# One attention stage reordered: B's logits computed once, C's and D's branches set between A's transposes and values

## The chip, the core and the metric

The kernel runs on one core of a Trainium2 chip. Each of the core's engines runs its own list of instructions: TensorE (PE in the rows; PEld is its weight load), VectorE (DVE), ScalarE (ACT), GpSimd (POOL) and SyncE (SP), which issues most of the DMAs. They meet only at semaphores. The metric is the device time of one execution in microseconds (us); lower is better.

## The reference, cut to what matters

Two layers of a decoder trunk, for a prompt of 512 tokens and 8 sample tokens that share the weights. Four branches read the same normalised input. Each is projected to 1024 features, multiplied by its own sigmoid gate (a 1024 x 1024 projection for each branch), and the four are summed.

```python
# A: four query heads, two key/value heads; the top 128 keys of each query are kept
score = einsum('bth,bthl->btl', iw, relu(einsum('bthd,bld->bthl', iq, kidx)))
_, idx = top_k(score, topk)
p = softmax(where(selected, q @ k * 64**-0.5, NEG)); o_a = p @ v
# B: stick-breaking, four heads
z = einsum('bthd,blhd->bhtl', q, k) * 64**-0.5
log_keep = where(mask, log_sigmoid(-z), 0)
after = cumsum(log_keep, reverse) - log_keep
a = where(mask, exp(log_sigmoid(z) + after), 0); o_b = a @ v
# C and D are scans over chunks; they are finished before the stage that is changed here
merged = g0*(o_a @ w_br_a) + g1*(o_b @ w_br_b) + g2*(o_c @ w_br_c) + g3*(o_d @ w_br_d)
```

B's exponent is `z` plus a reverse cumulative sum of the masked softplus of `z`, taken negative.

## The kernel before

Everything is float32. A dense tile of weights (1024 x 128) is split in a leading part (ACT, line 1018, in `WH`) and a rest (DVE or POOL, lines 1321 and 1745, in `WL`), and `dense_split` multiplies 8 chunks by 3 products by 2 halves of 260 tokens, 48 matmuls (line 490). Weights arrive in a ring of four slots; a slot is free when PE has counted `tile_used`.

The stage that the change touches is the prompt's attention, once in each layer. Its loop runs over t = 0 to 3. In step t, A handles the 128 queries of block t against w = 128 (t + 1) keys, and B handles its head t for all 512 queries, as four blocks of keys (`bblock`, 512, 384, 256 and 128 columns wide). Between these PE computes the gates of C and D for two chunks of 128 features (four `gate_cd`, into PSUM banks 2 and 3) and the matching projections of C and D (four `branch_cd`, into the same two banks). All orders are written out by hand, each engine's as a list with waits.

PE's order in step t: four index products (line 844); B's logits (851); two of A's logits (`attend`, 859); `gate_cd` 0 and 1; a wait for the masked softplus; the cumulative sums of B (869, 871), each followed by the logits of the block once more, added to the same bank (851); `gate_cd` 2; B's values (880); A's two other logits; `gate_cd` 3; four `branch_cd` (825); then for each head of A the transposes of its probabilities (897), and one head behind them its values (543).

The partners: ACT takes relu of the index products (1187), computes B's softplus term in three passes (1190 to 1192), B's weights (1199), A's exponentials (1204), the gates' tanh (1208), and copies A's transposed probabilities back for PE (1220). DVE forms the index score (1619, 1622), finds the top 128 in 16 rounds of max and replace (1650, 1651; none in step 0), adds up the softplus (1633, seen as line 1300), scales the gates out of banks 2 and 3 (`gate_cd_scaled`, 1613, seen as line 1297), finishes A's softmax, and multiplies each `branch_cd` by its gate out of the same banks (1668, seen as 1300). So each `gate_cd` waits for DVE to have taken the one before (`f_raw`), and each `branch_cd` for DVE to have taken the one before (`f_used`). In the 16 rounds, the softplus stands ahead of round 5, and the scalings of gates 0 and 1 ahead of rounds 7 and 12:

```python
for k in range(TOPK_P // 8):
    if k == 5:
        softplus()
    elif k == 7:
        gate_cd_scaled(t, 0)
    elif k == 12:
        gate_cd_scaled(t, 1)
    do(v_.max(M8[:, :], score))
    do(v_.match_replace(score, M8[:, :], score, TAKEN))
```

In step 0 DVE also rebuilds the rest part `XL` of the normalised input, eight operations on 128 x 520, because the scans before have used its memory. POOL masks (1732, 1793), splits weights (1745) and adds C and D (1807).

Of the kernel before, what the change touches and what calls it, by code (L numbers as in the profile page):

```python
# [11 lines left out]
NPR = 512  # L12
# [4 lines left out]
KD = DM // 128  # L17
# [79 lines left out]
def trunk_kernel(nc, x_in, pages, consts, vecs, states, c_state, d_state, k_c, v_c,  # L97
# [9 lines left out]
    with ctx:  # L107
# [373 lines left out]
        def _(pe):  # L481
# [54 lines left out]
            def values(l, t, h):  # L536

                q0 = 64 * (h // 2)
                if t and h == 0:
                    pe.wait_ge(*a_out.nth(l, t - 1))  # L540
                pe.wait_ge(*at_trc.nth(l, 4 * t + h))
                for j in range(t + 1):
                    ins = mm(PS[q0:q0 + 64, 6, 256 + 128 * (h % 2):384 + 128 * (h % 2)], TM[:, T_AV, j, q0:q0 + 64],
                             PTR[h % 2][:, 128 * j:128 * j + 128], start=j == 0, stop=j == t)
                finish(ins, at_pv)
# [23 lines left out]
            for l in range(L):  # L569
# [246 lines left out]
                def branch_cd(t, i):  # L816
                    nb = FIRST["fill"] + 5 * t + 4
                    if i == 0:
                        pe.wait_ge(*full(l, nb))
                        pe.wait_ge(*f_raw.nth(l, 4 * t + 3))  # L820
                    else:
                        pe.wait_ge(*f_used.nth(l, 4 * t + i - 1))
                    for k in range(2):
                        for a in range(2):
                            ins = mm(PS[:, 2 + a, 0:HALF],  # L825
                                     slot(l, nb)[:, 256 * i + 128 * k:256 * i + 128 * k + 128],
                                     F[:, (CQ, DZ)[i % 2] + k, a * HALF:(a + 1) * HALF], start=k == 0, stop=k == 1)
                    finish(ins, tile_used if i == 3 else f_done)
# [4 lines left out]
                for s in (c_out, d_out):  # L833
                    pe.wait_ge(*s.nth(l, 1))
                for t in range(NT):
# [14 lines left out]
                    def logits(i, start):  # L850
                        return mm(bblock(i), F[r0:r0 + 64, BK + c, 128 * i:128 * i + 128],  # L851
                                  F[r0:r0 + 64, BQ + c, 128 * i:NPR], start=start, stop=True)
                    for i in range(NT):
                        ins = logits(i, True)
                    finish(ins, z_done)

                    def attend(h):
                        q0 = 64 * (h // 2)
                        finish(mm(PS[:, h % 2, 0:w], F[q0:q0 + 64, AQ + h % 2, 128 * t:128 * t + 128],
                                  F[q0:q0 + 64, AK, 0:w], start=True, stop=True), at_qk)  # L860
# [7 lines left out]
                    for i in range(NT):  # L868
                        mm(bblock(i), kc(C_NTRI), BA1[:, OFF[i]:OFF[i] + NPR - 128 * i], start=True, stop=False)
                        for j in range(i + 1, NT):  # L870
                            mm(bblock(i, 128 * (j - i)), kc(C_NONE),
                               BA1[:, OFF[j]:OFF[j] + NPR - 128 * j], start=False, stop=False)
                        ins = logits(i, False)
# [13 lines left out]
                    for i in range(4):  # L887
                        branch_cd(t, i)
                    for h in range(4):
                        q0 = 64 * (h // 2)  # L890
# [9 lines left out]
                        if h:  # L900
                            values(l, t, h - 1)
                    values(l, t, 3)
# [78 lines left out]
        def _(act):  # L981
# [42 lines left out]
            for l in range(L):  # L1024
# [157 lines left out]
                for t in range(NT):  # L1182
# [18 lines left out]
                    split(l, m + 4)  # L1201
                    for h in range(4):
                        act.wait_ge(*at_max.nth(l, 4 * t + h))
                        do(A(S[:, h, 0:w], S[:, h, 0:w], ACT.Exp, bias=MX[:, h:h + 1], scale=0.125,
                             accum_out=MX[:, 4 + h:5 + h]), at_exp)
                    for i in range(4):
                        act.wait_ge(*f_raw.nth(l, 4 * t + i))
                        do(A(gate_at(t, i), gate_at(t, i), ACT.Tanh, scale=0.5), f_tanh)
                    split(l, m + 5)
                    if t % 2:  # L1210
                        act.wait_ge(*pv_done.nth(l, t))
                        do(A(F[:, BQ + t // 2, 0:NPR], PS[:, 7, :], ACT.Copy), b_out)
                    if t == 0:
                        act.wait_ge(stored.sem, N_STORES_MID[l])
# [72 lines left out]
        def _(dve):  # L1287
# [76 lines left out]
            for l in range(L):  # L1364
# [249 lines left out]

                for t in range(NT):
# [8 lines left out]
                    if t == 0:  # L1624
                        for k in range(KD):
                            stt(XL[:, k, :], X[:, k, :], V[:, l, V_NPRE + k:V_NPRE + k + 1], XH[:, k, :].bitcast(f32),
                                ALU.mult, ALU.subtract, xl_again)
# [14 lines left out]
                    else:  # L1642
                        for k in range(TOPK_P // 8):
                            if k == 5:
                                softplus()
                            elif k == 7:
                                gate_cd_scaled(t, 0)
                            elif k == 12:
                                gate_cd_scaled(t, 1)
# [320 lines left out]
```

## Time and profile before

| | |
|---|---|
| median of 3 runs | 2766.27 us (2757.04 to 2773.68) |
| the profiled execution: its own time | 2763.92 us |
| its span, first to last instruction | 2762.2 us |
| mean granted TensorE clock (1 is 2.4 GHz, 0.5 is 1.2 GHz) | 0.912 |
| PE busy | 2428.7 us (88%) |
| DVE, ACT, POOL busy | 1417.8 (51%), 904.2 (33%), 345.9 us (13%) |
| attention stage of layer 0, of layer 1 | about 497.8 to 766.0, 1869.6 to 2138.0 us from the start |

Busy time of PE is that of overlapping, pipelined matmuls, so 88% is no peak. In rows in order of time, the number in square brackets is how long the engine sat idle before the group, with what released it.

### The profile page before, as it was taken

To read this page: it belongs to the slowest core of one execution; us is meant where nothing else is said; L and a number is where in the kernel's file an instruction comes from. 1 tells how busy PE (TensorE), PEld (TensorE's weight loads), DVE (VectorE), ACT (ScalarE), POOL (GpSimd) and SP (SyncE) were. 2 spreads that over 40 slices of the span, in tenths; PEclk is the share of its full clock that TensorE was granted. 3 is DMA by queue.
4 is the path that set the end of the run, shared out by engine and by line. 5 is a ranking of instruction groups with operands and counts; after the bars stand their busy time and mean duration, and the time that the engine had idled before them with its cause. 6 is when DMAs were issued, how large, how long until landed. Compare 5 with 4: busy or idle time off the path is not lost.

```text
span 2762.2 us, 40540 instructions
## 1 busy us (share of the span) xinstructions
PE 2428.7 (88%) x15956; PEld 2022.7 (73%) x15956; DVE 1417.8 (51%) x2215; ACT 904.2 (33%) x1288; POOL 345.9 (13%) x412
## 2 busy tenths in 40 slices
PE   6899778788899899999898996987888997999996
PEld 6659424566699789989784683345666997999896
DVE  3329444445634577772342484444455445777723
ACT  3023424333322444442220225133333224444421
POOL 0016132222200000000000251222222000000000
PEclk9999658899999899999999996578999998999998
DMA  4362330111122122222215424201111221222221
GB/s 156 116 205 83 109 126 1 49 47 39 39 77 92 54 85 93 92 93 79 104 65 161 151 72 144 85 0 57 46 39 39 85 85 62 79 91 92 93 85 62
DMA packets 85184, 229.85 MB, mean 83 GB/s; under 512 B 10498, under 2 KB 28034, under 8 KB 84354
## 3 DMA queue, kind: packets, MB, share of 16 engines
q1 hardware_dynamic: 72434, 204.16, 22.3%
q10 hardware_dynamic: 12560, 23.11, 2.6%
q8 instruction: 126, 2.06, 0.3%
q14 instruction: 64, 0.52, 0.1%
HBM read 216.68 MB, written 10.55 MB: 82 GB/s over the span
## 4 chain that ended last, share of the span: by engine, by line
PE 73%; DVE 15%; ACT 6%; DMA 2%; issue 2%; ACTq 1%; POOL 1%; SPq 0%; DVEq 0%; POOLq 0%
PE PS L490 49%; PE PS L968 3%; PE PS L825 2%; DVE T L1425 2%; DVE M L1424 2%; DMA R<-k_c 2%; DVE S L1300 2%; DVE F L1300 2%; PE PS L782 1%; PE PS L851 1%; PE PS L555 1%; PE PS L522 1%; PE PS L919 1%; PE PS L718 1%; DVE WL L1321 1%
## 5 line engine op out<-in xcount | busy, mean ns | idle before, releaser
L490 PE MATMUL PS<-XH,WH 128*128 128x260 f32 x3616 | 760.6, 292 | 114.9 <-DVE WL L1321 43.4
L490 PE MATMUL PS<-XL,WH 128*128 128x260 f32 x3616 | 741.0, 287 | 5.3 <-issue 5.3
L490 PE MATMUL PS<-XH,WL 128*128 128x260 f32 x3616 | 740.0, 287 | 0.0
L490 PEld LDWEIGHTS PS<-XH,WH 128*128 128x128 f32 x3616 | 576.9, 194 | 133.8 <-issue 93.0
L1018 ACT ACTIVATE WH<-R 128x1024 fp32r<-128x1024 f32 x270 | 286.0, 1059 | 1043.1 <-PE PS L490 848.9
L490 PEld LDWEIGHTS PS<-XL,WH 128*128 128x128 f32 x3616 | 570.6, 193 | 5.7 <-issue 5.7
L490 PEld LDWEIGHTS PS<-XH,WL 128*128 128x128 f32 x3616 | 569.7, 193 | 0.0
L1321 DVE TENSOR_TENSOR WL<-R,WH 128x1024 fp32r<-128x1024 f32 x204 | 250.8, 1230 | 386.3 <-ACT WH L1018 385.5
L1745 POOL TENSOR_TENSOR WL<-R,WH 128x1024 fp32r<-128x1024 f32 x66 | 156.6, 2373 | 467.5 <-ACT WH L1018 466.7
L490 PE MATMUL PS<-FR,WH 128*128 128x260 f32 x1024 | 186.3, 284 | 0.0
L1297 DVE TENSOR_TENSOR S<-PS,RB 128x520 f32<-128x520 f32 x120 | 83.9, 700 | 176.0 <-PE PS L490 174.4
L490 PEld LDWEIGHTS PS<-FR,WH 128*128 128x128 f32 x1024 | 150.1, 189 | 0.1
L1300 DVE SCALAR_TENSOR_TENSOR S<-S,V 128x510 f32<-128x510 f32 (+1 forms) x176 | 132.2, 751 | 6.2
L1297 DVE TENSOR_TENSOR F<-PS,RB 128x520 f32<-128x520 f32 x56 | 39.2, 700 | 150.2 <-PE PS L490 149.6
L1741 POOL TENSOR_SCALAR F<-F 128x1040 f32<-128x1040 f32 x2 | 5.7, 2852 | 773.8 <-DVE F L1297 773.8
L825 PE MATMUL PS<-F,R 128*128 128x260 f32 x256 | 64.4, 395 | 28.9 <-DVE F L1300 21.3
L968 PE MATMUL PS<-F,R 128*128 128x260 f32 x384 | 87.5, 383 | 0.8 <-PE PS L968 0.8
L1424 DVE MAX8 M<-T 8x8 f32<-8x1025 f32 x64 | 77.9, 1217 | 19.6 <-ACT T L1051 17.4
L968 PEld LDWEIGHTS PS<-F,R 128*128 128x128 f32 x384 | 71.5, 190 | 11.6 <-issue 1.6
L825 PEld LDWEIGHTS PS<-F,R 128*128 128x128 f32 x256 | 46.0, 189 | 45.8 <-DVE F L1300 31.1
L1425 DVE MATCH_REPLACE8 T<-M,T 8x1025 f32<-8x1025 f32 x64 | 76.8, 1200 | 0.0
L1264 ACT ACTIVATE S<-S,V 128x520 f32<-128x520 f32 x88 | 72.5, 824 | 3.2
(306 smaller groups left out, 2901.4 us busy)
## 6 DMA issues: line engine op xcount, KB each, us to landing
R<-w_up SPq DMA_DIRECT2D x88, 512.0 KB, 3.2
R<-w_gate SPq DMA_DIRECT2D x64, 512.0 KB, 3.2
R<-w_proj SPq DMA_DIRECT2D x58, 512.0 KB, 3.2
R<-v_c SPq DMA_DIRECT2D x128, 192.0 KB, 2.4
R<-w_down SPq DMA_DIRECT2D x44, 512.0 KB, 3.2
R<-k_c SPq DMA_DIRECT2D x72, 256.0 KB, 3.2
R<-k_c ACTq DMA_DIRECT2D x56, 256.0 KB, 3.6
R<-w_br SPq DMA_DIRECT2D x16, 512.0 KB, 3.2
```

What stands on the lines that cost most here:

```text
L490: i = mm(PS[:, bank + a, 0:HALF], p[:, w, k * 128:(k + 1) * 128], x[:, a * HALF:(a + 1) * HALF], start=first and p is WH and x is hi, stop ...
L522: ins = mm(PS[:, 4 + a, 0:HALF], kc(C_ONE), S[:, k % 2, a * HALF:(a + 1) * HALF], start=k == 0, stop=k == KD - 1)
L825: ins = mm(PS[:, 2 + a, 0:HALF], slot(l, nb)[:, 256 * i + 128 * k:256 * i + 128 * k + 128], F[:, (CQ, DZ)[i % 2] + k, a * HALF:(a + 1) * H ...
L968: ins = mm(PS[:, bank + a, 0:HALF], slot(l, n)[:, 128 * e:128 * e + 128], F[:, q, a * HALF:(a + 1) * HALF], start=k == 0, stop=k == JF - 1)
L1018: do(A(WH[:, half(l, m), :], slot(l, SPLIT[m]), ACT.Copy), w_hi)
L1264: do(A(S[:, 2 + g, :], S[:, g, :], ACT.Identity, bias=V[:, l, V_FCB + ch:V_FCB + ch + 1], scale=V[:, l, V_FCW + 3 * ch + 2:V_FCW + 3 * ch ...
L1297: do(v_.tensor_tensor(out, a, b, op), s)
L1300: do(v_.scalar_tensor_tensor(out, a, sc, b, o0, o1), s)
L1321: v_.tensor_tensor(WL[:, half(l, m), :], slot(l, SPLIT[m]), WH[:, half(l, m), :].bitcast(f32), ALU.subtract).then_inc(w_lo.sem, 1)
L1424: do(v_.max(M8[0:8, :], T[0:8, 0:PAST + 1]))
L1425: do(v_.match_replace(T[0:8, 0:PAST + 1], M8[0:8, :], T[0:8, 0:PAST + 1], TAKEN))
L1745: g_.tensor_tensor(WL[:, half(l, m), :], slot(l, SPLIT[m]), WH[:, half(l, m), :].bitcast(f32), ALU.subtract).then_inc(w_lo_p.sem, 1)
```

## The change

It has six parts. (1) In the cumulative sums, B's logits are not computed a second time: the sums are added onto the logits that have stood in the banks since the start of the step. (2) A's heads are walked in another order, so that neighbours in the loop lie in different halves of the partitions: `attend` takes rows 0 to 63 and 64 to 127 in turn, and `values` handles two heads at once, whose matmuls alternate between output partitions 0 to 63 and 64 to 127. (3) PE's tail of a step becomes: branch 0, transposes of two heads, branch 1, values of these two, branch 2, transposes of the other two, branch 3, their values. (4) ACT computes tanh of gates 0, 1 and 2 ahead of A's exponentials or between them, and B's output copy and the next split ahead of tanh of gate 3. (5) In DVE's rounds, softplus stands ahead of round 4, gates 0 and 1 ahead of rounds 5 and 10. (6) DVE rebuilds `XL` before the loop, and PE waits for the outputs of C and D at the first `branch_cd` and no longer before the loop.

```diff
-            def values(l, t, h):
-                q0 = 64 * (h // 2)
-                if t and h == 0:
+            def values(l, t, p):
+                if t and p == 0:
                     pe.wait_ge(*a_out.nth(l, t - 1))
-                pe.wait_ge(*at_trc.nth(l, 4 * t + h))
+                for h in range(2 * p, 2 * p + 2):
+                    pe.wait_ge(*at_trc.nth(l, 4 * t + h))
                 for j in range(t + 1):
-                    ins = mm(PS[q0:q0 + 64, 6, 256 + 128 * (h % 2):384 + 128 * (h % 2)], TM[:, T_AV, j, q0:q0 + 64],
-                             PTR[h % 2][:, 128 * j:128 * j + 128], start=j == 0, stop=j == t)
-                finish(ins, at_pv)
+                    for h in range(2 * p, 2 * p + 2):
+                        q0 = 64 * (h % 2)
+                        ins = mm(PS[q0:q0 + 64, 6, 256 + 128 * p:384 + 128 * p], TM[:, T_AV, j, q0:q0 + 64],
+                                 PTR[h % 2][:, 128 * j:128 * j + 128], start=j == 0, stop=j == t)
+                        if j == t:
+                            finish(ins, at_pv)
...
                 def branch_cd(t, i):
...
+                        if t == 0:
+                            pe.wait_ge(*c_out.nth(l, 1))
+                            pe.wait_ge(*d_out.nth(l, 1))
...
                 pe.wait_ge(*scaled.nth(l, 1))
-                for s in (c_out, d_out):
-                    pe.wait_ge(*s.nth(l, 1))
...
-                        q0 = 64 * (h // 2)
-                        finish(mm(PS[:, h % 2, 0:w], F[q0:q0 + 64, AQ + h % 2, 128 * t:128 * t + 128],
+                        q0 = 64 * (h % 2)
+                        finish(mm(PS[:, h % 2, 0:w], F[q0:q0 + 64, AQ + h // 2, 128 * t:128 * t + 128],
...
                     for i in range(NT):
-                        mm(bblock(i), kc(C_NTRI), BA1[:, OFF[i]:OFF[i] + NPR - 128 * i], start=True, stop=False)
+                        ins = mm(bblock(i), kc(C_NTRI), BA1[:, OFF[i]:OFF[i] + NPR - 128 * i], start=False,
+                                 stop=i == NT - 1, skip_group_check=True)
                         for j in range(i + 1, NT):
-                            mm(bblock(i, 128 * (j - i)), kc(C_NONE),
-                               BA1[:, OFF[j]:OFF[j] + NPR - 128 * j], start=False, stop=False)
-                        ins = logits(i, False)
+                            ins = mm(bblock(i, 128 * (j - i)), kc(C_NONE),
+                                     BA1[:, OFF[j]:OFF[j] + NPR - 128 * j], start=False, stop=j == NT - 1,
+                                     skip_group_check=True)
                     finish(ins, ac_done)
...
-                    for i in range(4):
-                        branch_cd(t, i)
-                    for h in range(4):
-                        q0 = 64 * (h // 2)
+                    def turn(h):
                         pe.wait_ge(*at_norm.nth(l, 4 * t + h))
...
                         finish(ins, at_tr)
-                        if h:
-                            values(l, t, h - 1)
-                    values(l, t, 3)
+                    branch_cd(t, 0)
+                    turn(0)
+                    turn(1)
+                    branch_cd(t, 1)
+                    values(l, t, 0)
+                    branch_cd(t, 2)
+                    turn(2)
+                    turn(3)
+                    branch_cd(t, 3)
+                    values(l, t, 1)
...
+                    gate_cd_tanh(0)
+                    gate_cd_tanh(1)
                     for h in range(4):
+                        if h == 2:
+                            gate_cd_tanh(2)
                         act.wait_ge(*at_max.nth(l, 4 * t + h))
...
-                    for i in range(4):
-                        act.wait_ge(*f_raw.nth(l, 4 * t + i))
-                        do(A(gate_at(t, i), gate_at(t, i), ACT.Tanh, scale=0.5), f_tanh)
-                    split(l, m + 5)
                     if t % 2:
                         act.wait_ge(*pv_done.nth(l, t))
                         do(A(F[:, BQ + t // 2, 0:NPR], PS[:, 7, :], ACT.Copy), b_out)
+                    split(l, m + 5)
+                    gate_cd_tanh(3)
...
+                for k in range(KD):
+                    stt(XL[:, k, :], X[:, k, :], V[:, l, V_NPRE + k:V_NPRE + k + 1], XH[:, k, :].bitcast(f32),
+                        ALU.mult, ALU.subtract, xl_again)
                 for t in range(NT):
...
                         for k in range(TOPK_P // 8):
-                            if k == 5:
+                            if k == 4:
                                 softplus()
-                            elif k == 7:
+                            elif k == 5:
                                 gate_cd_scaled(t, 0)
-                            elif k == 12:
+                            elif k == 10:
                                 gate_cd_scaled(t, 1)
```

## Rows read from the trace of the kernel before

**Rows 1.** The page's chain that ended last, share of the span by engine.

```profile
PE 73%; DVE 15%; ACT 6%; DMA 2%; issue 2%; ACTq 1%; POOL 1%; SPq 0%; DVEq 0%; POOLq 0%
```

**Rows 2.** Stretches: length, busy us of PE, PEld, DVE, ACT, POOL (instructions), clock, DMA.

```profile
497.80:766.00 268.20, 223.49 (x1267) 176.37 (x1268) 137.20 (x303) 95.02 (x156) 63.62 (x62) 0.93 0.14 47
1869.60:2138.00 268.40, 223.86 (x1266) 176.45 (x1267) 137.21 (x303) 95.01 (x156) 63.61 (x62) 0.93 0.14 47
```

**Rows 3.** The chain in order of time, layer 0, step 1: start, us, what.

```profile
595.02 1.05 PE PS L851 x2
...
600.30 0.42 PE PS L851 x2
600.72 5.95 PE PS L490 x48
```

**Rows 4.** PE in order of time: first matmuls of gate 1, steps 1 to 3.

```profile
584.64 0.80 PE L490 MATMUL PS<-XH,WH 128*128 128x260 f32 x2 [4.58 <-DVE F L1297]
...
648.17 0.80 PE L490 MATMUL PS<-XH,WH 128*128 128x260 f32 x2 [4.79 <-DVE F L1297]
...
715.16 0.80 PE L490 MATMUL PS<-XH,WH 128*128 128x260 f32 x2 [6.51 <-DVE F L1297]
```

**Rows 5.** DVE in order of time: softplus in step 1, four rows of step 3.

```profile
579.82 2.06 DVE L1300 SCALAR_TENSOR_TENSOR F<-PS,F 128x512 f32<-128x512 f32 x4 [1.51 <-ACT F L1192]
...
709.27 2.07 DVE L1300 SCALAR_TENSOR_TENSOR F<-PS,F 128x512 f32<-128x512 f32 x4
...
714.41 0.70 DVE L1297 TENSOR_TENSOR F<-PS,RB 128x520 f32<-128x520 f32 x1
...
733.49 0.15 DVE L1303 TENSOR_SCALAR MX<-MX 128x1 f32<-128x1 f32 x1
```

**Rows 6.** PE in order of time: tail of step 0, tail of step 3.

```profile
555.92 1.99 PE L825 MATMUL PS<-F,R 128*128 128x260 f32 x8 [0.95 <-DVE F L1297]
...
569.29 0.70 PE L844 MATMUL PS<-F 64*128 64x256 f32 x4
...
747.96 1.99 PE L825 MATMUL PS<-F,R 128*128 128x260 f32 x8 [0.96 <-DVE F L1297]
750.84 2.02 PE L825 MATMUL PS<-F,R 128*128 128x260 f32 x8 [0.89 <-DVE F L1300]
...
758.52 1.04 PE L897 MATMUL PS<-K,S 128*128 128x128 f32 x8
...
764.05 1.04 PE L543 MATMUL PS<-S,TM 128*64 128x128 f32 x8
```

**Rows 7.** PE in order of time: pairs in different halves, pairs in one half.

```profile
357.20 1.97 PE L714 MATMUL PS<-B,K 8*64 8x512 f32 x4 [10.83 <-POOL B L1764]
...
695.76 1.13 PE L844 MATMUL PS<-F 64*128 64x512 f32 x4
...
739.07 1.98 PE L859 MATMUL PS<-F 64*128 64x512 f32 x4
```

**Rows 8.** Stretches, columns as in Rows 2: during line 714's first pair.

```profile
357.20:359.10 1.90, 1.90 (x5) 0.29 (x5) 0.00 (x0) 1.87 (x3) 1.80 (x2) 0.50 0.00 0
```

**Rows 9.** DVE and POOL in order of time, start of the stage in layer 0.

```profile
512.18 3.22 DVE L1300 SCALAR_TENSOR_TENSOR F<-S,SMT,F 128x128 f32<-128x128 f32 x3
515.43 6.33 DVE L1300 SCALAR_TENSOR_TENSOR XL<-X,V,XH 128x520 fp32r<-128x520 f32 x8
...
523.39 2.07 DVE L1300 SCALAR_TENSOR_TENSOR F<-PS,F 128x512 f32<-128x512 f32 x4 [1.36 <-ACT F L1192]
...
509.71 4.76 POOL L1745 TENSOR_TENSOR WL<-R,WH 128x1024 fp32r<-128x1024 f32 x2 [22.78 <-ACT WH L1018]
```

**Rows 10.** PE in order of time: a pause in another stage, and the matmuls behind it.

```profile
1230.10 0.47 PE L490 MATMUL PS<-XH,WH 128*128 128x260 f32 x2 [3.43 <-DVE FR L1297]
...
1231.44 0.64 PE L490 MATMUL PS<-XH,WL 128*128 128x260 f32 x2
```

**Rows 11.** Stretches, columns as in Rows 2: gate 1 after its pause, step 1.

```profile
584.60:589.50 4.90, 4.86 (x22) 4.86 (x23) 4.57 (x15) 0.00 (x0) 1.24 (x1) 0.50 0.01 2
```

More of the change, by code:

```diff
@@ L848, in _ @@
                         pe.wait_ge(*a_out.nth(l, t - 1))
-                    def logits(i, start):
-                        return mm(bblock(i), F[r0:r0 + 64, BK + c, 128 * i:128 * i + 128],
-                                  F[r0:r0 + 64, BQ + c, 128 * i:NPR], start=start, stop=True)
                     for i in range(NT):
-                        ins = logits(i, True)
+                        ins = mm(bblock(i), F[r0:r0 + 64, BK + c, 128 * i:128 * i + 128],
+                                 F[r0:r0 + 64, BQ + c, 128 * i:NPR], start=i < 3, stop=True, skip_group_check=True)
                     finish(ins, z_done)
                     def attend(h):
-                        q0 = 64 * (h // 2)
-                        finish(mm(PS[:, h % 2, 0:w], F[q0:q0 + 64, AQ + h % 2, 128 * t:128 * t + 128],
+                        q0 = 64 * (h % 2)
+                        finish(mm(PS[:, h % 2, 0:w], F[q0:q0 + 64, AQ + h // 2, 128 * t:128 * t + 128],
                                   F[q0:q0 + 64, AK, 0:w], start=True, stop=True), at_qk)
@@ L1201, in _, with gate_cd_tanh @@
                     split(l, m + 4)
+                    def gate_cd_tanh(i):
+                        act.wait_ge(*f_raw.nth(l, 4 * t + i))
+                        do(A(gate_at(t, i), gate_at(t, i), ACT.Tanh, scale=0.5), f_tanh)
+                    gate_cd_tanh(0)
+                    gate_cd_tanh(1)
                     for h in range(4):
+                        if h == 2:
+                            gate_cd_tanh(2)
                         act.wait_ge(*at_max.nth(l, 4 * t + h))
@@ L1623, in _ @@
                             ix_sum if h == 3 else dve_own)
[L1624 to L1627, printed above, removed]
                     def softplus():
```

## The prediction

> **What bounds the kernel now.** First the chain of work that ended last: PE has 73% of it, DVE 15%, ACT 6% [rows 1]. So a change pays where it shortens PE's list, or a wait inside it. Then the stretches: the stage is as long in layer 1 as in layer 0, 268.4 and 268.2 us, and in both PE is busy for 223 us of it, DVE for 137, ACT for 95, at a granted clock of 0.93 [rows 2]. Two equal stages mean that one layer can be costed and doubled. Neither DVE nor ACT fills the stage, so PE sets the pace, and the 45 us in which it is idle are handovers to the other two. Third, PE in order of time shows where these lie. Gate 1 of steps 1 to 3 starts after pauses of 4.58, 4.79 and 6.51 us, each ended by DVE's line 1297, the scaling of gate 0 [rows 4]. Each branch after the first starts 0.89 us after the one before, waiting for DVE's product [rows 6]. Last, the chain in order of time passes through B's repeated logits, with nothing beside them [rows 3].
>
> **Logits once.** The reader should look at line 851 among the sums: 1.05 us for the block of 512 columns, 0.42 for that of 128 [rows 3]. Between them the cost is linear in columns, so four blocks take 4 x 0.735 = 2.94 us. The sums themselves stay, and whether they start a bank or add to it is the same number of matmuls. Behind them ACT and POOL prepare B's weights while PE runs gate 2, 5.95 us [rows 3]; both shift together, so no cover is lost. Gain: 2.94 a step.
>
> **Rounds 4, 5 and 10.** What PE waits for in gate 1 is softplus, two rounds, and the scaling. In step 1 softplus itself waited 1.51 us for ACT and began at 579.82 [rows 5], so a place one round ahead brings it no forward. But one round instead of two follows it: from its end, 581.88, to PE's start, 584.64, less a scaling of 0.70 and some 0.1 of handover, two rounds take 2.0 us. Gain 0.98. In step 3 softplus began without a wait [rows 5]: it moves up by one round, and one round less follows. Two rounds are 714.41 - 711.34 = 3.07 us. Gain 3.0 (1.5, should ACT's term come a round later than needed). Step 2 has rounds between these; its gain lies between one round and two, 1.25 and 2.5, of which I take 1.9.
>
> The price of the move is at the other end: six rounds instead of four now follow gate 1's scaling. In step 3 DVE had head 1's maximum at 733.64 [rows 5], and PE asked for it at 739.07 [rows 7]: 5.4 us of cover. PE is about to save 2.94 + 3.0 + 0.85 = 6.8 us ahead of that point, so there the cover goes and DVE decides. Gate 3 can't start before the maximum and gate 2's scaling, 733.64 + 0.70 = 734.34; it started at 741.05 [rows 7]. Step 3 can gain 6.7 at the most, and less by what DVE waits for gate 1 at round 10. With gate 1 partly at half clock, where 4.9 us cost 2.45 [rows 11], I put that wait between 0 and 1.6 and take 0.4: 6.3 for step 3 in all.
>
> **Pairs of logits.** Four 512-column matmuls whose inputs lie in two halves of the partitions take 1.13 us (line 844), and four in one half 1.98 (line 859) [rows 7]. The second pair of A's logits goes from the one kind to the other: 0.85 in step 3 (inside the 6.3), in proportion to columns 0.21, 0.43, 0.64 in steps 0 to 2. The first pair stands ahead of gate 0, and what it saves ends in gate 1's pause: nothing.
>
> **The tail.** From branch 0 to the next step's first product: 13.37 us in step 0 and, to the end of the last values at 765.08, 17.12 in step 3 [rows 6]; steps 1 and 2 in line with these, 14.6 and 15.9. New: four branches of 2.02 and three pauses of 0.89 [rows 6] make 10.75. Into the pauses go two heads' transposes, two heads' values, and two heads' transposes again. Eight transposes are 1.04 us in step 3, and one head's eight value matmuls 1.04 [rows 6]. If the values of two heads overlap, each of the pieces is 0.26 (t + 1): hidden in steps 0 to 2, 0.15 over in step 3. The last pair of values stays in the open. That is 11.0, 11.3, 11.5 and 12.2 us, a gain of 2.4, 3.3, 4.4 and 4.9. Each of the four pieces brings a handover that no row shows: between 0 and 0.4 us, twice the 0.2 that a pause of 0.89 leaves beside a product of 0.70 (the scaling's time for the same shape [rows 5]). I take 0.1 each, 1.6 a layer. The tail gives 15.0 - 1.6 = 13.4.
>
> Do the values overlap? The nearest rows are line 714's: four 512-column matmuls into two halves of the output in 1.97 us at half clock [rows 7, 8], against 1.98 at full clock for four in one half. At equal clock that is half the time. I take overlap.
>
> What stands in the queues: on ACT the copies of the transposed probabilities now lie behind a split and gate 3's tanh, but PE has a branch of 2.02 us to run before it needs them. The three tanh ahead of A's exponentials, some 2.1 us if each is like DVE's 0.70 on the same shape [rows 5], delay A's softmax under gate 3's 5.95. Without that cover they would delay the scaling of gate 3, and PE's first branch.
>
> **The start of the stage.** `XL` goes ahead of the score, 6.33 us of DVE [rows 9]. There it meets POOL's two splits, 4.76 us. Three 128-column operations beside these took 1.07 us each, more than the 0.79 of an `XL` operation four times as wide [rows 9], so DVE is held up by them. Held up for both, counted from POOL's start at 509.71, `XL` ends at 520.8 and the four score operations, at no more than 0.79 each, at 524.0; DVE waits for ACT's term until 523.39 anyway [rows 9]. So at worst 0.6 us shows, and I take nothing. The splits may wait in turn for one `XL` operation each: 0 taken, 1.6 a layer at most. PE's earlier start gains nothing, since ACT's relu still waits for D's output.
>
> **Sum of a layer.** Steps 0 to 3 ahead of the tail: 2.94 + 0.21 = 3.15; 2.94 + 0.98 + 0.43 = 4.35; 2.94 + 1.9 + 0.64 = 5.48; 6.3. Together 19.3, with the tail 32.7, twice 65.4. The profiled execution took 2763.92 us: 2698.5. The median of the runs lies 2.4 above the profiled time; I predict 2698.
>
> **The rivals.** (a) *The clock stays up.* In gate 1 the clock was at 0.5 for 4.9 us after its pause of 4.58 [rows 4, 11]. I leave this loss in the sum, because a pause of 3.43 us elsewhere was also followed by matmuls at 0.64 in place of 0.4 [rows 10], and the new pauses are 3.6, some 2.9 and 3.5. If they are short enough, step 1 gains 2.45 more and step 2 some 1.2: 7.3 in two layers, 2691.
>
> (b) *The values of a pair don't overlap.* Both use all 128 input partitions, which line 714 (8 partitions) doesn't [rows 7]. Then two heads' values are 0.52 (t + 1): the pause is exceeded by 0.15, 0.67 and 1.04 us more in steps 1 to 3, and the last pair costs 0.26 (t + 1) more. That is 4.5 a layer, 2707. The Trainium skill, in "TensorE: Matmul & The Clock Gate", Part 3, says that a weight load overlaps running matmuls only if its row group is another one, and here it is the same for both heads. By that page this rival is the forecast, and the time 2707; no run yet shows this shape.
>
> (c) *ACT or DVE is late in the tail.* Should the copies miss the values, each step loses up to a tanh and a split, by DVE's 0.70 for 520 columns [rows 5] some 0.7 and 1.4 for 1024: 2.1 a step, 17 in all, 2715.
>
> (d) *The time is handed back* in the gates of A and B behind the stage: 2764. Against it: they are PE's own dense work, and the chain is PE's for 73% [rows 1].
>
> (e) *Slower.* The one mechanism I see is the clock: more and shorter pauses, and PE granted 0.5 over whole gates. A matmul pair then takes 0.64 for 0.4 pipelined; a gate of 5.95 us would take nearly twice that. It decides when over 65.4 / 5.95 = 11 of the 32 gates run wholly at 0.5; with all of them the time is 2698 + 190 = 2888. Against it: the pauses shrink, and the stage already has 0.93 [rows 2].
>
> **How the numbers follow.** The forecast 0.45, (a) 0.2, (b) 0.17, (c) 0.1, (d) 0.03, (e) 0.03, and 0.02 for what I don't see. About 0.5%, 14 us, is what can be told from no change. Faster, then, 0.94, within 0.5% 0.03, slower 0.03. The range: below, (a) with handovers at 0 (3.2) and DVE without a wait (0.8): 2687. Above, (b) with handovers at 0.4 (9.6), DVE's wait at 1.6 (2.4) and the splits (3.2) would be 2722. Runs of before lie 7 to 9 us around their median, so 2683 to 2722.
>
> **What would show it.** Line 851 with 64 matmuls where it had 128, the sums about 5 us long; pauses before gate 1 near 3.6, 2.9 and 3.5; PE waiting in step 3 for DVE's maximum before A's last logits; branches still 2.9 us apart with transposes and values between them; value matmuls of two heads starting together, or, for (b), one behind the other. A pause before gate 2 or longer gaps between branches would make the prediction wrong, and so would a lower clock in the stage.

## The result, and the profile after

The changed kernel takes 2692.75 us, the median of 4 runs (2684.39 to 2695.82), against 2765.34 for the kernel before on the same chip: a ratio of 0.9733, with a 95% interval of 0.9695 to 0.977. The forecast was 2698. The profiled execution took 2695.82 us, with a span of 2694.1.

First the page's chain that ended last, share of the span by engine:

```profile
PE 72%; DVE 15%; ACT 7%; DMA 2%; issue 2%; ACTq 1%; POOL 1%; SPq 0%; DVEq 0%; POOLq 0%
```

The stage in the view of stretches, columns as in [rows 2]. Here and below it runs from its first matmul to the first gate of A and B behind the last branch.

```profile
497.36:729.52 232.16, 200.40 (x1232) 165.63 (x1233) 138.76 (x303) 95.12 (x156) 63.51 (x62) 0.92 0.16 52
1838.16:2070.84 232.68, 200.94 (x1232) 165.98 (x1233) 139.05 (x303) 95.12 (x156) 63.50 (x62) 0.92 0.16 52
```

PE still sets the end, and the two stages are still equal. Each is 36 us shorter than in [rows 2]: 23 us of PE's busy time are gone, and some 13 us of its waits. DVE is busy for 1.6 to 1.8 us longer than before, with the same 303 instructions.

PE in order of time, from the first index product of step 1 to its first branch, and the starts of gate 1 in steps 2 and 3:

```profile
562.56 0.70 PE L848 MATMUL PS<-F 64*128 64x256 f32 x4
...
576.94 0.80 PE L490 MATMUL PS<-XH,WH 128*128 128x260 f32 x2 [3.49 <-DVE F L1312]
...
585.19 1.02 PE L872 MATMUL PS<-F,K 128*128 128x512 f32 x2
...
589.44 0.49 PE L490 MATMUL PS<-XH,WH 128*128 128x260 f32 x2
...
605.29 1.99 PE L831 MATMUL PS<-F,R 128*128 128x260 f32 x8 [0.95 <-DVE F L1312]
...
631.29 0.80 PE L490 MATMUL PS<-XH,WH 128*128 128x260 f32 x2 [3.55 <-DVE F L1312]
...
687.81 0.58 PE L490 MATMUL PS<-XH,WH 128*128 128x260 f32 x2 [3.80 <-DVE F L1312]
```

The sums take 589.44 - 585.19 = 4.25 us, where they took 7.94 before. The pauses of [rows 4], 4.58, 4.79 and 6.51, are now 3.49, 3.55 and 3.80. Behind the one in step 1 the matmuls still run at half clock (0.80 for the first pair, 0.64 for those that follow).

The tail of step 0, and step 3 from A's second pair of logits to the end of the stage:

```profile
551.54 1.99 PE L831 MATMUL PS<-F,R 128*128 128x260 f32 x8 [0.95 <-DVE F L1312]
553.37 0.38 PE L899 MATMUL PS<-K,S 128*128 128x128 f32 x2
554.42 2.02 PE L831 MATMUL PS<-F,R 128*128 128x260 f32 x8 [0.67 <-DVE F L1315]
...
707.70 1.12 PE L862 MATMUL PS<-F 64*128 64x512 f32 x2
709.07 1.12 PE L862 MATMUL PS<-F 64*128 64x512 f32 x2 [0.24 <-DVE MX L1318]
...
717.10 1.99 PE L831 MATMUL PS<-F,R 128*128 128x260 f32 x8 [0.95 <-DVE F L1312]
718.92 1.04 PE L899 MATMUL PS<-K,S 128*128 128x128 f32 x8
719.98 2.02 PE L831 MATMUL PS<-F,R 128*128 128x260 f32 x8
721.93 0.32 PE L545 MATMUL PS<-F,TM 128*64 128x128 f32 x1
721.93 0.32 PE L545 MATMUL PS<-S,TM 128*64 128x128 f32 x1
...
722.95 2.02 PE L831 MATMUL PS<-F,R 128*128 128x260 f32 x8
...
729.52 0.47 PE L490 MATMUL PS<-XH,WH 128*128 128x260 f32 x2 [0.61 <-ACT F L1237]
```

Branches start 2.88 to 2.97 us apart, where [rows 6] have 2.88, with transposes and values now between them; in step 3 the values fill the pause of 0.89 with 0.06 us over. Value matmuls of the two heads start together, at 721.93.

The parts of a stage, as differences of starts in such rows (a front runs from the first index product to branch 0, in step 0 from gate 0; a tail from branch 0 to the next step), layer 0:

| part | before | after | gain | predicted |
|---|---|---|---|---|
| start, to gate 0 of step 0 | 19.05 | 18.61 | 0.44 | 0 |
| front of step 0 | 39.07 | 35.57 | 3.50 | 3.15 |
| front of step 1 | 47.64 | 42.73 | 4.91 | 4.35 |
| front of step 2 | 48.44 | 43.45 | 4.99 | 5.48 |
| front of step 3 | 52.21 | 45.67 | 6.54 | 6.3 |
| four tails | 61.45 | 46.12 | 15.33 | 13.4 |
| the stage | 267.86 | 232.16 | 35.7 | 32.7 |

### The profile page after: what moved, and what is told of

It reads as the page before. It is cut to its first block, busy times and chain, and to the rows that moved or that the text cites. A ratio compares the mean times of both kernels' runs of the same rounds, so it can differ in the third digit from the quotient of the medians.

```text
span 2694.1 us, 40422 instructions
## 1 busy us (share of the span) xinstructions
PE 2381.6 (88%) x15892; PEld 2002.7 (74%) x15892; DVE 1421.3 (53%) x2215; ACT 905.1 (34%) x1288; POOL 347.6 (13%) x412
## 4 chain that ended last, share of the span: by engine, by line
PE 72%; DVE 15%; ACT 7%; DMA 2%; issue 2%; ACTq 1%; POOL 1%; SPq 0%; DVEq 0%; POOLq 0%
PE PS L490 50%; PE PS L977 3%; PE PS L831 2%; DVE T L1440 2%; DVE M L1439 2%; DVE S L1315 2%; DMA R<-k_c 2%; DVE F L1315 2%; PE PS L785 1%; PE PS L928 1%; PE PS L522 1%; PE PS L721 1%; PE PS L558 1%; DVE S L1312 1%; DVE WL L1336 1%
## 5 line engine op out<-in xcount | busy, mean ns | idle before, releaser
L977 PEld LDWEIGHTS PS<-F,R 128*128 128x128 f32 x384 | 71.5, 190 | 11.6 <-issue 1.6
L623 PE MATMUL PS<-R,QB 128*32 128x256 f32 x256 | 73.1, 411 | 0.0
```

The source lines that it names most:

```text
L623: ins = mm(PS[64:96, bank, col:col + 256], QB[:, c, b, :], rec[:, 1 + c], start=st and c == 0, stop=end and c == 1, skip_group_check=True)
L977: ins = mm(PS[:, bank + a, 0:HALF], slot(l, n)[:, 128 * e:128 * e + 128], F[:, q, a * HALF:(a + 1) * HALF], start=k == 0, stop=k == JF - 1)
```

## The experiments

Ten runs, each an edit of the changed kernel, and the changed kernel once more. Ratios are to the kernel before on the same chip; the runs were made on several chips, so medians of different rows are compared through their ratios.

| edit | stage, layers 0 and 1 | median us | ratio (95%) |
|---|---|---|---|
| none | 232.16, 232.68 | 2692.75 | 0.9733 (0.9695 to 0.977) |
| none, once more | 232.12, 232.11 | 2683.02 | 0.9725 (0.9691 to 0.976) |
| logits between the sums again | 245.92, 248.58 | 2715.97 | 0.9819 (0.9777 to 0.9862) |
| logits twice, in one go | 237.31, 240.62 | 2693.42 (1 run) | none |
| branches first | 248.05, 249.58 | 2726.0 | 0.9877 (0.9833 to 0.992) |
| values one head behind the other | 233.46, 233.47 | 2697.16 | 0.9758 (0.972 to 0.9796) |
| rounds 5, 7, 12 again | 236.59, 235.66 | 2703.21 | 0.9774 (0.9734 to 0.9814) |
| `XL` and waits in the old places | 232.16, 232.68 | 2687.23 | 0.9741 (0.9719 to 0.9764) |
| ACT's old order | 232.17, 232.69 | 2690.98 | 0.9737 (0.9711 to 0.9764) |
| gate 0 ahead of softplus | 232.32, 232.36 | 2698.56 | 0.9757 (0.9725 to 0.9788) |
| the same, but not in step 3 | 228.14, 228.43 | 2674.73 | 0.9694 (0.9671 to 0.9717) |
| and POOL's split behind the bias | 224.51, 224.52 | 2672.98 | 0.9693 (0.9658 to 0.9728) |

The stage repeats to 0.04 us in layer 0 and to 0.6 in layer 1; the whole execution doesn't. The unaltered kernel in two profiled executions, in the view of stretches, both from 1450 to 1570 us, first the one above, then the one once more:

```profile
1450.00:1570.00 120.00, 110.37 (x700) 70.99 (x700) 42.38 (x53) 25.99 (x33) 27.31 (x15) 0.94 0.53 171
```

```profile
1450.00:1570.00 120.00, 111.32 (x756) 75.30 (x754) 48.50 (x60) 27.65 (x35) 31.51 (x17) 1.00 0.55 176
```

The clock granted was 0.94 in one and 1.00 in the other, outside the stage; the spans are 2694.1 and 2677.7, while the stages differ by 0.6 us in sum. So the effect of an edit is read from the stage, and a median that moves by less than 10 us tells little.

> The changed kernel once more, unaltered, to compare the others with on one chip: 2688 to 2696 us, the stage 232.2 and 232.7 us.

The median came 5 us under the lower end of that, the stages 0.1 and 0.6 us under.

**Logits between the sums again.**

```diff
-                        ins = mm(bblock(i), kc(C_NTRI), BA1[:, OFF[i]:OFF[i] + NPR - 128 * i], start=False,
-                                 stop=i == NT - 1, skip_group_check=True)
+                        mm(bblock(i), kc(C_NTRI), BA1[:, OFF[i]:OFF[i] + NPR - 128 * i], start=True, stop=False)
...
+                        ins = logits(i, False)
```

> The changed kernel with one part undone: B's logits are computed a second time behind each block of the sums. My prediction priced the repeat at 2.94 us a step. The trace of the changed kernel shows the sums with the gate behind them starting 4.26 us after the sums begin, against 7.94 before, so the repeat would cost 3.68: the 2.94 of the logits and 0.74 for entering and leaving matmuls of 64 rows between matmuls of 128 rows. Theory (3.68): a step's sums go back to about 7.9 us, and with some 0.3 us less in step 3, where PE now waits for DVE, the kernel gets 2 x (3 x 3.7 + 3.4) = 29 us longer, about 2722. Rival (2.94, the rest was something else in the change): sums of 7.2 us and 23 us, about 2716. Rival (DVE decides the steps): 0 to 10 us.

PE in order of time in this kernel, the sums of step 1:

```profile
598.86 1.02 PE L874 MATMUL PS<-F,K 128*128 128x512 f32 x2
...
601.11 1.12 PE L856 MATMUL PS<-F 64*128 64x512 f32 x2
...
606.39 0.49 PE L856 MATMUL PS<-F 64*128 64x128 f32 x2
606.81 0.51 PE L490 MATMUL PS<-XH,WH 128*128 128x260 f32 x2
```

The sums take 606.81 - 598.86 = 7.95 us again, so the repeat costs 3.7 a step, not the 2.94 of the prediction. The fronts of layer 0 grow by 3.68, 3.72, 3.59 and, in step 3, where DVE is close behind, by 2.45; the stages by 13.8 and 15.9.

**Logits twice, in one go.** Why 3.7? The repeat is set ahead of the sums:

```diff
                     for i in range(NT):
+                        mm(bblock(i), F[r0:r0 + 64, BK + c, 128 * i:128 * i + 128],
+                           F[r0:r0 + 64, BQ + c, 128 * i:NPR], start=i < 3, stop=True, skip_group_check=True)
+                    for i in range(NT):
                         ins = mm(bblock(i), kc(C_NTRI), BA1[:, OFF[i]:OFF[i] + NPR - 128 * i], start=False,
```

> As the changed kernel, but B's four logits are computed a second time in one go ahead of the sums (they overwrite themselves), where the kernel before had them between the sums. The repeat between the sums cost 3.68 us a step, against 2.94 by columns alone. Theory: the 0.74 over is paid where 64-row matmuls stand between 128-row ones, at seven changes of shape, some 0.1 us each; in one go there are two changes, and the repeat costs 2.94 + 0.2 = 3.15: from the first repeated logit to gate 2 it takes 7.4 us. Rival: the 0.74 belongs to the repeat itself (its weights' load, the bank it writes): 7.9 us again.

PE in order of time, step 1 (line 872 is the repeat here, 875 the first sum):

```profile
584.77 2.42 PE L872 MATMUL PS<-F 64*128 64x512 f32 x8
587.12 1.12 PE L875 MATMUL PS<-F,K 128*128 128x512 f32 x2
...
591.48 0.48 PE L490 MATMUL PS<-XH,WH 128*128 128x260 f32 x2
```

Repeat and sums take 591.48 - 584.77 = 6.71 us, 2.46 more than the sums alone, where 7.4 was expected. The theory's direction held and its size did not: eight 64-row matmuls in a row take 2.35 us, less than the 2.94 that single rows had added up to, and standing between 128-row ones makes the same eight cost 1.2 us more. That the changes of shape are the reason isn't shown: here the repeat also overwrites the banks, where between the sums it adds to them.

The stage doesn't grow by four times 2.46, only by 5.2 and 7.9 us. In step 3 DVE is close behind, as in the run before. In step 2 of layer 0 the front doesn't grow at all, because gate 1 got another clock. Stretches from gate 1 to the sums in step 2, columns as in [rows 2]: before the change, after it, and in this run:

```profile
648.17:655.31 7.14, 7.14 (x48) 7.14 (x49) 5.89 (x15) 0.00 (x0) 0.65 (x1) 0.80 0.00 0
631.29:639.66 8.37, 8.37 (x48) 8.37 (x49) 5.90 (x15) 0.00 (x0) 1.93 (x1) 0.66 0.00 0
633.30:639.24 5.94, 5.94 (x49) 5.80 (x49) 5.63 (x15) 0.00 (x0) 1.95 (x1) 1.00 0.00 0
```

The work is the same 48 matmuls. The pause ahead of them is 3.55 us in the changed kernel and in this run, yet the clock granted behind it is 0.66 in one and 1.00 in the other, which is worth 2.4 us. So a front holds, besides its work, what the clock happens to do in it.

**Branches first.** The order of the tail is undone, the pairs stay.

```diff
-                    branch_cd(t, 0)
+                    for i in range(4):
+                        branch_cd(t, i)
                     turn(0)
                     turn(1)
-                    branch_cd(t, 1)
                     values(l, t, 0)
-                    branch_cd(t, 2)
                     turn(2)
                     turn(3)
-                    branch_cd(t, 3)
                     values(l, t, 1)
```

> The changed kernel with one part undone: the four branches of a step run one after the other, and transposes and values of both pairs behind them; the pairs stay. Theory (the pauses between branches hide this work): the tails go from 11.0, 11.2, 11.5 and 12.4 us to 10.75 for branches and pauses of 0.89 each, plus four pieces of 0.26 (t + 1) and waits for ACT's copies of some 0.5 each: 12.8, 13.8, 14.9 and 15.9, which is 11 a layer and 22 us in all, about 2715. Rival (the gain of the tail is from the pairs, and the order is worth little): under 6 us, about 2697.

The tails are 13.63, 14.61, 15.69 and 17.43 us, 0.8 to 1.5 more than expected: 61.36 in sum, against 61.45 before the change. So pairing the values gains nothing without the order, and the tail's gain hangs on the order. PE in order of time, the values of step 3:

```profile
739.93 0.29 PE L545 MATMUL PS<-F,TM 128*64 128x128 f32 x1 [1.02 <-ACT S L1233]
...
743.06 0.29 PE L545 MATMUL PS<-F,TM 128*64 128x128 f32 x1 [1.02 <-ACT S L1233]
```

Each pair of values waits 1.02 us for ACT's copies of both heads, where some 0.5 was expected, and that eats what the overlap saves. With a branch in between, the copies are done in time.

**Values one head behind the other.**

```diff
-                for j in range(t + 1):
-                    for h in range(2 * p, 2 * p + 2):
+                for h in range(2 * p, 2 * p + 2):
+                    for j in range(t + 1):
```

> The changed kernel with one edit: the values of a pair are computed one head after the other, not in turn. Theory (matmuls into two halves of the output run at the same time): a pair takes twice as long, 0.26 (t + 1) us more. The pair behind branch 3 shows all of it, 0.26 to 1.04; the pair between branches 1 and 2 shows what is over the pause that the changed kernel still has there, 0, 0.2, 0.8 and 1.0. Together 4.6 a layer, 9 us, about 2702, and in the trace the two heads' matmuls start one behind the other. Rival (weight loads of the same row group don't overlap, so turns gain nothing): no change, 2693.

The tails grow by 0.0, 0.0, 0.4 and 0.9 us, 1.3 a layer, less than expected. PE in order of time, step 3:

```profile
728.25 0.76 PE L545 MATMUL PS<-F,TM 128*64 128x128 f32 x5
728.75 0.32 PE L545 MATMUL PS<-S,TM 128*64 128x128 f32 x1
...
729.12 0.71 PE L545 MATMUL PS<-S,TM 128*64 128x128 f32 x5
729.76 2.02 PE L831 MATMUL PS<-F,R 128*128 128x260 f32 x8
```

The second head's matmuls into the other output half start while three of the first head's eight are still to start, and from there both alternate. So the two overlap in part even when they are listed one after the other, and taking turns is worth 729.76 - 728.25 = 1.51 against 722.95 - 721.93 = 1.02, 0.5 us a pair.

**Rounds 5, 7 and 12 again.**

```diff
-                            if k == 4:
+                            if k == 5:
                                 softplus()
-                            elif k == 5:
+                            elif k == 7:
                                 gate_cd_scaled(t, 0)
-                            elif k == 10:
+                            elif k == 12:
```

> The changed kernel with one part undone: softplus ahead of round 5, gates 0 and 1 ahead of rounds 7 and 12. Theory (gate 1 waits for softplus, the rounds behind it and the scaling): pauses before gate 1 go from 3.5, 3.55 and 3.8 us back to about 4.5, 4.8 and 6.6, which is 1.0 in step 1, 1.2 in step 2, and in step 3 1.5 to 2.4 of 2.8, because PE meets DVE's maximum later anyway. About 4.2 a layer and 8 us in all, 2701, with some 2 us either way from the clock behind the pauses. Rival (DVE's 16 rounds set the steps, so where PE pauses is all one): under 3 us, 2694.

PE in order of time, gate 1 of the three steps:

```profile
577.32 0.80 PE L490 MATMUL PS<-XH,WH 128*128 128x260 f32 x2 [4.46 <-DVE F L1312]
...
633.14 0.80 PE L490 MATMUL PS<-XH,WH 128*128 128x260 f32 x2 [5.45 <-DVE F L1312]
...
691.61 0.80 PE L490 MATMUL PS<-XH,WH 128*128 128x260 f32 x2 [6.81 <-DVE F L1312]
```

The pauses return to 4.46, 5.45 and 6.81, and gate 1 starts 15.36, 16.65 and 19.40 us into its step, as before the change. (The pause of step 2 is longer than the 4.79 of then, because gate 0 starts 0.65 us earlier there.) The stage is 4.4 and 3.0 us longer: the theory held in sum, though step 1 lost 0.6 for the 1.0 expected and step 3 of layer 0 lost 3.1.

**`XL` and the waits in the old places; ACT's old order.** In the first, `XL` goes back between DVE's operations of step 0, and PE's waits for C's and D's outputs back ahead of the loop. In the second, all four tanh stand behind A's exponentials again, with the split behind them.

> As the changed kernel, but XL is written between the rounds of step 0's place as in the kernel before, and PE waits for C's and D's outputs ahead of the whole stage. Theory: the start of the stage is set by ACT's term for softplus, not by XL: the stage from its first matmul to gate 0 stays within 0.5 us of 18.61 and 18.93, XL takes 6.3 us for 8 in place of 10.26, and the time stays within 2 us of 2693. Rival: the 0.44 us a layer by which the start became shorter, and more with it, came from this part: the time rises by 1 to 4 us.

> As the changed kernel, but ACT's queue in the tail is as before: the three tanh behind all of A's exponentials, the split ahead of the copies of the transposed values. Theory: ACT has enough spare time in the tail that its order does not show: tails stay within 0.3 us of 11.02, 11.23, 11.45 and 12.42, and the time within 2 us of 2693. Rival: with branches first, PE asks for the first branch's products sooner than before, so tanh behind the exponentials comes late: 0.7 to 2.1 us a step at the first branch, 6 to 17 us in all, 2699 to 2710.

Both are null: the stages agree with the changed kernel's to 0.01 us, and so do the tails. The 0.44 us at the start are not from `XL`, then. They lie between B's first logit and gate 0 of step 0: 5.26 us before the change (511.60 to 516.86), 4.82 after it (511.15 to 515.97). Of what stands there the change touches only the first pair of A's logits, which runs at half clock: twice the 0.21 that was costed for a pair of that width would be 0.42. No run takes the pair alone back.

**Gate 0 ahead of softplus.** DVE scales gate 0 first, which is all that PE's gate 1 waits for.

```diff
                             if k == 4:
+                                gate_cd_scaled(t, 0)
                                 softplus()
-                            elif k == 5:
-                                gate_cd_scaled(t, 0)
```

> As the changed kernel, but DVE scales gate 0 ahead of softplus, both at round 4 (there: softplus at round 4, gate 0 at round 5); gate 1 stays at round 10. Theory: what PE waits for ahead of gate 1 is gate 0's scaling, which here no longer stands behind softplus and a round, so the pauses of 3.49, 3.55 and 3.80 us fall to 1.0 at most, and with them goes the half clock behind them (3.4 to 6.8 us in each of two steps, worth half of that). Steps 1 and 2 then gain 2.5 and 2.6 from the pause and up to 2.8 from the clock each; step 3 gains nothing, since DVE's maximum decides there, and loses some 0.6 where DVE waits for gate 0's matmuls: 10 us a layer with the clock, 5 without, and 2673 to 2683 us in place of 2693. Rival: another wait stands right behind, softplus's output for the sums or ACT's term, and PE pauses there instead, ahead of the sums: no gain, 2690 to 2695.

The first half came true: the pause ahead of gate 1 is 0.86 us in every step, no half clock follows, and the front of step 1 falls from 42.73 to 37.70. But step 2 loses 1.0 (44.47), step 3 3.85 (49.52), and the stage is as long as without the edit. PE in order of time, step 3, then DVE and POOL:

```profile
717.07 1.12 PE L862 MATMUL PS<-F 64*128 64x512 f32 x2 [3.35 <-DVE MX L1318]
718.71 2.07 PE L862 MATMUL PS<-F 64*128 64x512 f32 x2 [0.51 <-DVE MX L1318]
720.71 0.80 PE L490 MATMUL PS<-XH,WH 128*128 128x260 f32 x2
```

```profile
692.70 0.70 DVE L1312 TENSOR_TENSOR F<-PS,RB 128x520 f32<-128x520 f32 x1 [0.71 <-PE PS L490]
...
714.48 0.90 DVE L1318 TENSOR_SCALAR F<-F 128x512 f32<-128x512 f32 x1
```

```profile
712.74 2.35 POOL L1758 TENSOR_TENSOR WL<-R,WH 128x1024 fp32r<-128x1024 f32 x1 [4.22 <-ACT WH L1027]
```

PE's pause went from gate 1 to A's second pair of logits, behind DVE's maximum. DVE waits 0.71 us for gate 0, and its selection bias takes 0.90 us where it took 0.43. Worse, the half clock went along with the pause: here the second logits and the first part of gate 3 run under it, and nothing covers them. From gate 3 to branch 0 it takes 8.83 us where it took 6.98.

**The same, but not in step 3.**

```diff
                             if k == 4:
-                                gate_cd_scaled(t, 0)
+                                if t < NT - 1:
+                                    gate_cd_scaled(t, 0)
                                 softplus()
+                            elif k == 5 and t == NT - 1:
+                                gate_cd_scaled(t, 0)
```

> As e5, but step 3 keeps softplus ahead of gate 0 as in the changed kernel. Theory: in step 3 DVE is the bound, and a scaling of gate 0 placed early makes it wait for PE's gate 0 by some 0.6 us a layer, which this version saves: 1 us less than e5, 2672 to 2682, and a pause of 3.8 us ahead of gate 1 in step 3 that costs nothing. Rival: PE is the bound in step 3 as soon as its gate 1 is late: same time as e5 or up to 3 us more.

Step 3 is back at 45.66, the stage 4 us shorter than the changed kernel's. Step 2 stays at 44.44. PE, DVE and POOL in order of time there:

```profile
645.70 0.91 PE L862 MATMUL PS<-F 64*128 64x384 f32 x2 [3.01 <-DVE MX L1318]
...
648.11 0.80 PE L490 MATMUL PS<-XH,WH 128*128 128x260 f32 x2
```

```profile
641.87 2.41 DVE L1318 TENSOR_SCALAR F<-F 128x384 f32<-128x384 f32 x1
```

```profile
641.71 2.35 POOL L1761 TENSOR_TENSOR WL<-R,WH 128x1024 fp32r<-128x1024 f32 x1 [2.59 <-ACT WH L1027]
```

The bias ends at 644.28, 0.22 us after POOL's split; it began 0.16 us after it.

**And POOL's split behind the bias.**

```diff
+                    pool.wait_ge(*bias_ready.nth(l, t))
                     split(m + 4)
```

> As e8, but POOL starts the third split of a step only when DVE has written the selection bias. In e8 the bias of step 2 took 2.41 us in place of 0.36, from 641.87 to 644.28, while POOL's split ran from 641.71 to 644.06; PE then waited 3.01 us for A's maximum and gate 3 began at half clock. Theory: DVE's bias is held until POOL's split ends; with the split behind it the bias takes 0.36 us, PE's wait falls to about 1.0 us, no half clock follows, and step 2's front is 44.45 - 2.05 - 1.45 = 41.0 us: 3.5 us a layer less than e8, about 2668 us. Rival: the bias is long for another reason (DVE waits for something that the profile counts into it): it stays at 2.4 us and the time at 2675.

The same three engines:

```profile
644.09 0.91 PE L862 MATMUL PS<-F 64*128 64x384 f32 x2 [0.94 <-DVE MX L1318]
...
646.30 0.51 PE L490 MATMUL PS<-XH,WH 128*128 128x260 f32 x2
```

```profile
642.31 0.36 DVE L1318 TENSOR_SCALAR F<-F 128x384 f32<-128x384 f32 x1
```

```profile
642.80 2.36 POOL L1761 TENSOR_TENSOR WL<-R,WH 128x1024 fp32r<-128x1024 f32 x1 [3.25 <-DVE F L1318]
```

The bias takes 0.36 us, the wait 0.94, gate 3 runs at full clock, and the front of step 2 is 40.88, where 41.0 was expected. The stage is 7.6 us shorter than the changed kernel's on the same chip in either layer, 15 in two. The medians on one chip, 2672.98 and 2683.02, point the same way by 10; their intervals overlap, and against the run before it the median does not show the step at all.

## Why the prediction was right

**Where the time is** held: rivals (d) and (e) are out, with the whole gain found in two stages that are 36 us shorter. Their granted clock is 0.92 for 0.93, which in a shorter stage is no more time lost than before: 0.08 of 232 us, for 0.07 of 268.

**Logits once**: right, with a term too small, 2.94 for 3.7. The sum went by single rows of line 851, 1.05 and 0.42; it missed the 0.75 that the 128-row sums lose when the logits stand between them.

**Rounds 4, 5 and 10**: right. Counted from a step's first product, gate 1 starts 0.98, 1.88 and 3.03 us earlier in steps 1 to 3, for a forecast of 0.98, 1.9 and 3.0; that of step 2 had been taken between two bounds, so that it fits to 0.02 is luck. The pauses, forecast as 3.6, 2.9 and 3.5, are 3.49, 3.55 and 3.80. They are longer in steps 2 and 3 because gate 0 starts 0.65 and 0.31 us earlier there, behind A's first pair of logits: the prediction said that this saving ends in the pause, and left it out of the three figures.

That the front of step 2 gained 4.99 for 5.48 is the clock, which the sum took as unchanged. From gate 1 to the sums it takes 8.37 us where it took 7.14, at 0.66 in place of 0.80 (the rows beside the run with the logits twice, in one go).

Rival (a) did not come about in the changed kernel: gate 1 runs at half clock behind all three pauses. But the length of the pause alone doesn't decide it, as the 1.00 behind the same 3.55 us in that run shows. The runs with pauses of 0.86 us show what it would have been worth: 5.0 in step 1, of which 2.6 are the pause and 2.4 the clock, where (a) had 2.45.

**Step 3** was capped by DVE as forecast, and the gain is 6.54 for 6.3, but the terms of the bound were wrong and offset each other. PE runs one head's logits at 707.70, waits 0.24 us for the next maximum, and runs the last head's at 709.07. So the two don't run as a pair, and what stands between the maximum and gate 3 is one head's logits, 1.05 us, where the prediction had gate 2's scaling, 0.70. The 0.4 for a wait of DVE at round 10 was not needed: DVE's rows show none there.

**The tail**: 15.33, against 15.0 before handovers. The term for those, 1.6, should have been zero: ACT and DVE finish inside the branches. Rival (c) is out for the same reason, and ACT's order turned out not to matter. Rival (b) is out: the matmuls of two heads overlap. "TensorE: Matmul & The Clock Gate", Part 3, in the Trainium skill says that a weight load overlaps running matmuls only if its row group differs; the run with one head behind the other doesn't agree, since there matmuls with the same 128 rows and the other output half start 0.5 us after the first head's, before that head is done.

**The start**: nothing of `XL` shows, as forecast, and the reason was right. DVE in order of time after the change, step 0, then POOL beside `XL`:

```profile
508.05 10.26 DVE L1315 SCALAR_TENSOR_TENSOR XL<-X,V,XH 128x520 fp32r<-128x520 f32 x8
...
522.94 2.07 DVE L1315 SCALAR_TENSOR_TENSOR F<-PS,F 128x512 f32<-128x512 f32 x4 [2.31 <-ACT F L1201]
```

```profile
509.25 5.31 POOL L1759 TENSOR_TENSOR WL<-R,WH 128x1024 fp32r<-128x1024 f32 x2 [22.75 <-ACT WH L1027]
```

`XL` takes 10.26 us beside POOL's splits (6.33 in [rows 9]), and softplus still waits 2.31 us for ACT.

The errors don't point one way. In a layer the logits of steps 0 to 2 gave 2.3 us more than forecast, the tails 1.9, the start 0.4 and step 3 0.2; some 1.9 were lost in steps 0 to 2 between gate 0 and the sums, most of it to the clock. Together a layer gained 3 us more than forecast; so by the stages alone the profiled execution would have come out some 6 us under the forecast. It came out 2.7 under; the rest lies outside the stage, where two executions of one kernel differ by 16 us. The median came 5 under 2698, and that figure was low by the prediction's own words: its sum is for the profiled execution, and it put the median 2.4 above.

## What to carry to other kernels

A wait is only removed if the engine that it waited for has time to spare: gate 0 ahead of softplus gained 5 us in the step where DVE was early and lost 3.9 where it was already the bound, because the pause, and the half clock behind it, moved to work that nothing covers. Fill the waits of a chain with independent work rather than shorten that work: the order of the tail gave 15 us a layer, while pairing the values without the order gave 0.1. And read an edit of a few us from its stage, which repeats to half a us, not from a total that moves by 10, and look at the granted clock of the stretch beside it: it hid 2.4 us of added work in one step here.

## What had not been expected of the hardware

- One DVE operation on 128 x 384, the selection bias, took 2.41 us in place of 0.36 because a POOL split had begun 0.16 us before it; with the split behind it, the bias is back at 0.36, and the split takes 2.36 for 2.35. Beside POOL's second split in the same step each max keeps its 0.56 us. The Trainium skill, in "SBUF — State Buffer", section "Who interferes with whom", names `tensor_scalar` among the operations of DVE that can take the ports it shares with GpSimd, which whoever issues first holds for its whole instruction while the other is blocked. The run agrees: the bias that began second ended 0.22 us after the split.
- Eight 64-row matmuls cost 2.46 us ahead of the sums and 3.7 between them.
- The same pause of 3.55 us ahead of the same 48 matmuls was followed by a granted clock of 0.66 in one run and 1.00 in another.
- Matmuls of two heads into different output halves overlap from the middle of the first head on, even when they are listed one after the other.
